# A mixture-of-experts layer on one core: the router chain reordered, the PLE product moved into the expert loop

## The reference

```python
h = rmsnorm(x, g_ffn)
logits = h @ w_router + b_router                # (256, 32)
top_val, top_idx = lax.top_k(logits, 4)
top_w = softmax(top_val)
for each expert e, for the tokens that chose it:
    gu = h[tok] @ w1[e] + b1[e]                 # w1[e] 1024 x 2048
    gate = min(gu[:, :1024], 7); lin = clip(gu[:, 1024:], -7, 7)
    y[tok] += top_w * (((lin + 1) * gate * sigmoid(1.702 * gate)) @ w2[e] + b2[e])
x = x + y
x = x + sigmoid(rmsnorm(x, g_ple) @ w_ple_gate) * (p @ w_ple)      # the PLE term
```

## Time and profile before

| | |
|---|---|
| three runs | 1286.07, 1288.97, 1289.33 us; median 1288.97 |
| the profiled execution | 1289.37 us, its span 1287.1 us |
| PE, DVE, ACT, POOL busy | 90%, 22%, 16%, 3% of the span |
| mean granted PE clock | 0.984 |
| HBM read | 446.71 MB |

### The profile page before, as it was taken

The page is one execution under the profiler, slowest core; times in us unless marked ns, Lnnn a source line. Parts: engine busy times, 40 slices in busy tenths (PEclk is TensorE's granted clock), DMA queues, the critical chain, the costliest instruction groups (busy, mean ns, idle before and its releaser), DMA issues. The chain is left out here.

```text
span 1287.1 us, 15903 instructions
## 1 busy us (share of the span) xinstructions
PE 1164.7 (90%) x6370; PEld 479.2 (37%) x6370; DVE 281.4 (22%) x787; ACT 212.0 (16%) x430; POOL 34.1 (3%) x49
## 2 busy tenths in 40 slices
PE   7999999989999989899899999888988999989868
PEld 4455544444343333333333333333333333333333
DVE  1474533272121111112111111111111111111121
ACT  2323435022111111111111111111111111111110
POOL 2221100000000000000000000000000000000000
PEclk9999999997999999999999999999999999999989
DMA  9835041971999999999999999999999999999920
GB/s 294 290 131 196 1 131 54 378 291 39 429 428 429 427 431 428 428 429 427 430 429 428 429 427 430 428 429 429 427 430 428 429 429 427 430 428 429 429 87 33
DMA packets 51003, 448.07 MB, mean 348 GB/s; under 512 B 9233, under 2 KB 11638, under 8 KB 26310
## 3 DMA queue, kind: packets, MB, share of 16 engines
q1 hardware_dynamic: 49534, 442.24, 82.7%
q0 software_dynamic: 1264, 5.27, 1.2%
q10 hardware_dynamic: 184, 0.29, 0.1%
HBM read 446.71 MB, written 4.22 MB: 350 GB/s over the span
## 5 line engine op out<-in xcount | busy, mean ns | idle before, releaser
L340 PE MATMUL ps<-ring,wbuf 128*64 128x512 f32 x2048 | 464.4, 598 | 67.4 <-DMA ring<-in_w_e 67.0
L340 PEld LDWEIGHTS ps<-ring,wbuf 128*64 128x64 f32 x2048 | 139.9, 137 | 374.1 <-issue 229.0
L364 PE MATMUL ps<-ring,wbuf 128*64 128x512 f32 x1024 | 226.8, 595 | 21.6 <-ACT wbuf L379 21.6
L413 DVE TENSOR_SCALAR wbuf<-ps 128x512 f32<-128x512 f32 x32 | 22.1, 692 | 748.2 <-PE ps L340 748.2
L364 PEld LDWEIGHTS ps<-ring,wbuf 128*64 128x64 f32 x1024 | 70.7, 137 | 155.6 <-issue 127.9
L375 ACT ACTIVATE wbuf<-wbuf 128x512 f32<-128x512 f32 x32 | 20.1, 630 | 511.5 <-DVE wbuf L413 511.5
L1099 PE MATMUL ps<-wbuf,hT 128*128 128x512 f32 (+2 forms) x224 | 85.4, 540 | 1.0 <-ACT hT L571 1.0
L325 PE MATMUL ps<-wbuf 64*128 64x512 f32 x264 | 65.6, 615 | 0.7 <-ACT wbuf L381 0.7
L1181 PE MATMUL ps<-wbuf,hT 128*128 128x512 f32 x128 | 62.6, 619 | 0.0
L1099 PEld LDWEIGHTS ps<-wbuf,hT 128*128 128x128 f32 x224 | 42.1, 190 | 41.1 <-issue 37.9
L381 ACT COPY wbuf<-ps 128x512 f32<-128x512 f32 x32 | 18.8, 586 | 230.0 <-PE ps L364 230.0
(11 more groups left out here) (233 smaller groups left out, 699.9 us busy)
## 6 DMA issues: line engine op xcount, KB each, us to landing
ring<-in_w_e SPq DMA_DIRECT2D x192, 2048.0 KB, 24.3
wbuf<-in_w_in SPq DMA_DIRECT2D x9, 2048.0 KB, 9.0
wbuf<-in_w_out SPq DMA_DIRECT2D x1, 4096.0 KB, 14.1
rel_rows_repeated<-rel_rows POOLq DMA_DIRECT2D x1, 3072.0 KB, 20.7
wbuf<-in_w_ple_gate SPq DMA_DIRECT2D x1, 3072.0 KB, 17.5
ring<-rel_rows_repeated POOLq DMA_DIRECT2D x1, 2048.0 KB, 10.9
wbuf<-in_w_branch_a SPq DMA_DIRECT2D x2, 1024.0 KB, 9.8
wbuf<-in_w_branch_b SPq DMA_DIRECT2D x1, 2048.0 KB, 17.8
```

The lines of the kernel that those rows point to most:

```text
L340: l = mm((G, Lb)[n // 2][(n % 2) * SLOTS:(n % 2 + 1) * SLOTS, :], xeT[:, k, :], ring3[:, i, r * 2 * DFF + n * 512:r * 2 * DFF + (n + 1) * ...
L364: l = mm(O[n * SLOTS:(n + 1) * SLOTS, :], actT[:, r, h * SLOTS:(h + 1) * SLOTS], ring3[:, i, r * DM + n * 512:r * DM + (n + 1) * 512], sta ...
L413: d.tensor_scalar(gc, ps[0][:, :], LIMIT, None, ALU.min).then_inc(s["gc_ready"], 1)
```

## The change

The attention part, the last part after the loop and all sizes stay. In the stretch between:

- `g_ffn` is multiplied once into the router weights `wr` on DVE; the eight small ACT evacuations of a tile become two plain copies (`x_copy`).
- Residual add, squares and the split into parts go by halves of 512. ACT makes part 0 straight from `x` with the scale (`hi`) and part 1 (`mid`), DVE the remainders and part 2. POOL keeps one instruction, `pow`.
- PE does `x_rows(1)`, `router(0)` and `x_rows(2)` ahead of `w_out(3)`.
- The mask comes from `match_replace` on the top four (`choose`), the rank counts are bfloat16 products. Exponential and `Wt` come after the one-hot matrix of expert 0.
- `b_e2` is loaded into the rows of `oe`, and the first visit's scatter adds it; DVE sets the four output banks to zero instead (`y_init`), after the first `take_rows`.
- The PLE product runs between the twelfth and the thirteenth visit (`ple_pe`, `ple_act`), so the loop is written twice, for 12 and for 20 visits.
- SP: `w_ple_gate` is loaded in 5/8 and 3/8 in place of 6/8 and 2/8, the later part behind `rt_ps` 2 and `hp_ready` 4.

The core of the diff:

```diff
@@ expert_pe @@
+            if a is first:
+                te.wait_ge(wt_ready, 1)
+                for t in range(TT):
+                    l = tr(T[:, t * P:(t + 1) * P], Wt[:, t, :], ident)
+                l.then_inc(s["wst_ps"], 1)
...
+            if a is first:
+                te.wait_ge(y_init, 1)
+                with te.Fori(0, PLE_AFTER) as it:
+                    visit(it)
+                ple_pe(te)
+                with te.Fori(PLE_AFTER, NE) as it:
+                    visit(it)
...
+        def ple_pe(te):
+            te.wait_ge(ld_p, 16)
+            for k in range(2):
+                for t in range(TT):
+                    l = tr(ps[3][:, k * SEQ + t * P:k * SEQ + (t + 1) * P], pin[:, t, k * P:(k + 1) * P], ident)
+            l.then_inc(pt_ps, 1)
+            te.wait_ge(pt_ev, 1)
+            te.wait_ge(ld_ple, 16)
+            for i in range(4):
+                t, n = i // 2, (i % 2) * 512
+                if i == 3:
+                    te.wait_ge(pl_ev, 1)
+                for k in range(2):
+                    l = mm(ps[(0, 1, 3, 0)[i]][:, :], pT[:, k, t * P:(t + 1) * P], wple[:, k, n:n + 512], start=k == 0, stop=k == 1)
+                l.then_inc(pl_ps, 1)
+            te.wait_ge(pl_ev, 4)
@@ expert_dve @@
             take_rows()
+            if a is first:
+                ve.wait_ge(t_ev, NT + 8)
+                for b in range(4, 8):
+                    l = d.memset(ps[b][:, :], 0.0)
+                l.then_inc(y_init, 1)
@@ sync @@
+                for n in range(2):
+                    sp.dma_start(oe[n * SLOTS:n * SLOTS + NE, :], io["b_e2"][0][:, n * 512:(n + 1) * 512]).then_inc(ld_be2, 16)
...
-                sp.wait_ge(hp_ready, 2)
-                sp.dma_start(wple_g[:, 0:2], w_gate[:, 0:2]).then_inc(ld_ple_gate, 16)
+                sp.wait_ge(rt_ps, 2)
+                sp.wait_ge(hp_ready, 4)
+                sp.dma_start(wple_g[:, 0:3], w_gate[:, 0:3]).then_inc(ld_ple_gate, 16)
@@ scalar @@
+                for n in range(4):
+                    merged_copy(n)
+                x_copy(0)
+                x_copy(1)
+                hi(0)
+                mid(0)
+                x_copy(2)
+                x_copy(3)
+                hi(1)
+                mid(1)
                 sc.wait_ge(lg_ready, 1)
...
+                a.activation(ex, lgx, ACT.Exp).then_inc(rt_exp, 1)
@@ vector @@
+                d.tensor_tensor(wr, wr, bc(gT[:, 16:24], NE), ALU.mult).then_inc(wr_ready, 1)
...
+                def choose(t):
                     ve.wait_ge(rt_ps, t + 1)
                     ch(d.scalar_tensor_tensor(lg[:, t, :], ps[6 + t][:, 0:NE], rs[:, t:t + 1], br, ALU.mult, ALU.add))
                     ch(d.max(top8[:, t, :], lg[:, t, :]))
+                    ch(d.tensor_scalar(lgx[:, t, :], lg[:, t, :], top8[:, t, 0:1], None, ALU.subtract))
+                    ch(d.memset(top8[:, t, TOPK:8], -TAKEN))
+                    ch(d.match_replace(lg[:, t, :], top8[:, t, :], lg[:, t, :], TAKEN))
+                    d.tensor_scalar(Mb[:, t, :], lg[:, t, :], (BLOCKED + TAKEN) / 2, None, ALU.is_lt).then_inc(m_ready, 1)
+
+                add(0)
+                add(1)
+                square(0)
+                square(1)
+                add(2)
+                square(2)
+                for n in range(2):
+                    remainder(0, n)
+                for n in range(2):
+                    last_part(0, n)
+                choose(0)
+                add(3)
+                square(3)
+                remainder(1, 0)
+                remainder(1, 1)
+                choose(1)
+                last_part(1, 0)
+                last_part(1, 1)
+                ve.wait_ge(m_ready, 2)
+                d.tensor_copy(Mt, Mb).then_inc(lg_ready, 1)
...
@@ tensor @@
                 w_out(2)
                 x_rows(0)
+                x_rows(1)
+                te.wait_ge(wr_ready, 1)
+                router(0, range(KT))
+                x_rows(2)
                 w_out(3)
-                x_rows(1)
-                x_rows(2)
...
+                router(1, range(4))
                 x_rows(3)
+                router(1, range(4, KT))
+                te.wait_ge(m_ready, 2)
```

More of the change, by code:

```diff
@@ L329, in expert_pe, with visit @@
             gather()
-            with te.Fori(0, a["visits"]) as it:
+            if a is first:
[3 more added lines that the diff above has]
+                l.then_inc(s["wst_ps"], 1)
+            def visit(it):
                 te.wait_ge(s["sel_ready"], it + 1)
@@ L366, in expert_pe @@
                     l.then_inc(s["pieces_used"], 1)
+            if a is first:
[5 more added lines that the diff above has]
+                    visit(it)
+            else:
+                with te.Fori(0, a["visits"]) as it:
+                    visit(it)
             te.wait_ge(s["out_ready"], a["visits"] + 1)
@@ L381, in expert_act @@
                 nc.scalar.copy(oe, ps[2][:, :]).then_inc(s["out_ready"], 1)
+            if a is first:
+                with sc.Fori(0, PLE_AFTER) as it:
+                    visit(it)
+                ple_act(sc)
+                with sc.Fori(PLE_AFTER, NE) as it:
+                    visit(it)
+            else:
+                with sc.Fori(0, a["visits"]) as it:
+                    visit(it)
         def expert_dve(ve, a):
@@ L696, in _, with merged_copy @@
                     a.activation(gates[:, t, :], gates[:, t, :], ACT.Sigmoid).then_inc(gates_ready, 1)
[L697 to L703, removed]
+                def merged_copy(n):
                     k = NT + n
@@ L707, in _, with x_copy @@
                     a.copy(hTv[:, k0:k0 + 4, t * P:(t + 1) * P], ps[4 + k % 2][:, :].rearrange("p (k t) -> p k t", k=4)).then_inc(t_ev, 1)
-                part(1, 0, 1)
-                part(2, 0, 2)
-                for n in range(4):
+                def x_copy(n):
                     k = NT + 4 + n
@@ new lines, in add, with square @@
+                def add(i):
+                    t, c = i // 2, slice((i % 2) * 512, (i % 2 + 1) * 512)
+                    ve.wait_ge(wo_ps, i + 1)
+                    d.tensor_tensor(x[:, t, c], ps[i][:, :], x[:, t, c], ALU.add).then_inc(x2_ready, 1)
+                def square(i):
+                    t, c = i // 2, slice((i % 2) * 512, (i % 2 + 1) * 512)
+                    ve.wait_ge(x2_ready, i + 1)
+                    l = d.tensor_tensor_reduce(out=xr[t][:, c], in0=x[:, t, c], in1=x[:, t, c], scale=1.0 / DM,
+                                               scalar=EPS if i % 2 == 0 else sm2[:, t, 0:1],
+                                               op0=ALU.mult, op1=ALU.add, accum_out=sm2[:, t, 0:1] if i % 2 == 0 else ssx[:, t:t + 1])
+                    if i % 2 == 0:
+                        ch(l)
+                    else:
+                        l.then_inc(f_sq, 1)
@@ new lines, in _ @@
+                ve.wait_ge(m_ready, 2)
+                d.tensor_copy(Mt, Mb).then_inc(lg_ready, 1)
+                ve.wait_ge(lg_ready, 1)
+                ve.wait_ge(rk_ps, 1)
+                ch(d.scalar_tensor_tensor(rank[:, :, 0:NE], ps[7][:, P:P + TT * NE].rearrange("p (t e) -> p t e", t=TT), 1.0, Mt, ALU.add, ALU.mult))
+                i1 = iota1[:, 0, :]
+                for t in range(TT):
+                    l = d.tensor_scalar(S[:, t, :], i1, rank[:, t, 0:1], None, ALU.is_equal)
+                l.then_inc(first["s"]["s_ready"], 1)
@@ L1013, in _ @@
-                ve.wait_ge(wt_ready, 1)
-                second_remainder(1)
-                ve.wait_ge(rk_ps, 1)
                 for t in range(TT):
-                    ch(d.scalar_tensor_tensor(rank[:, t, 0:NE], ps[7][:, t * NE:(t + 1) * NE], 1.0, Mt[:, t, :], ALU.add, ALU.mult))
+                    l = d.tensor_scalar(Wt[:, t, :].rearrange("p (r e) -> p r e", r=ROUNDS), bm(ex[:, t, :], ROUNDS), sm2[:, t, 1:2], None, ALU.mult)
+                l.then_inc(wt_ready, 1)
+                for t in range(TT):
```

195 lines of the change are left out of this document (75 added, 120 removed).

## The result

| | before | after |
|---|---|---|
| median of five runs | 1289.33 us (1286.07 to 1290.23) | 1277.39 us (1274.59 to 1281.20) |
| ratio | | 0.9913, 95% interval 0.9894 to 0.9931 |
| profiled execution, span | 1289.37, 1287.1 us | 1279.43, 1277.6 us |

The change makes the kernel 0.9% faster, between 9 and 14 us by the interval. A second set of six runs gave 1277.07 and a ratio of 0.9902 (0.9879 to 0.9924). The forecast was 1275.0, within 1270.7 to 1280.8: the direction and the range hold, and the point is 2.4 us too low.

The account below looks back on a forecast made before the run. The chain up to the first used piece of expert 1, then the even weight stream, sets the end. 14.8 us earlier less 0.45 for the clock gives 1289.37 - 14.35 = 1275.0 us, range 1270.7 to 1280.8.

Parts of the forecast that it names:

- rival of a slower stream: In the loop the stream's rate falls; 0.6 us more a visit gives 1293.6 us; chance 3%.
- that of no gain: Something other than the first used piece starts the stream, so the earlier chain is swallowed: 1289 us; chance 4%.
- Step 1: Chain up to the end of `w_out(3)`: it ends at 283.3 us, 4.2 us later than before.
- the clock falls earlier: Clock falls at the start of `w_out(3)`, which ends 1.9 to 2.8 us later: 1276.9 to 1277.8 us; chance 10%.
- Step 2: From the end of `w_out(3)` to the gather: 7.75 us, gather starting at 291.05 instead of 307.77.
- Step 3: From the gather to the first piece: zeroings 1.95 us, L340 at 297.25 instead of 312.03, 14.8 us earlier.
- Step 4: PE's clock at the first piece: starts at the lower level, rises 4.6 us after the start; 0.45 us lost.
- Step 5: PLE product in the loop: PE uses no piece for 9.1 us, hidden by queued loads; cost nothing.
- lead of 16.9: Smallest time in the loop from a piece's issue to its own transfer's start, 16.9 us, more than 9.1.
- The handover: Two stalls of 5.1 us as PE leaves one loop and enters the other: 1277.4 us; chance 6%.
- Step 6: Transfers ahead of the loop: last 1.5 MB of `w_ple_gate` done by about 297 us, `b_e2` needed near 312; cost nothing.
- 14.35: Net gain forecast up to the first piece, in us: 14.8 from the earlier chain less 0.45 for the clock.

Follow-up runs that it names:

- fourfold product: Changed kernel with three more PLE products (24 logical products, results overwritten) in the gap after the twelfth visit; median 1287.18 us, ratio to before 0.9992.
- second profile: Profiled execution of the changed kernel run once more with no edit; median of that set 1277.07 us, ratio to before 0.9902.
- first profile: Profiled execution of the changed kernel in its first measurement, 1279.43 us; median of that set 1277.39 us, ratio to before 0.9913.
- the same with filling: Kernel before with the PLE product moved into the loop and fifteen unread products of constants in PE's gaps; median 1278.88 us, ratio to before 0.9915.

## Why the prediction was right

- **The bound was right.** Every profile has the same loop, 922.7 to 923.4 us, whatever lies ahead of it, but for the fourfold product. So the end of the loop moves with the first load, microsecond for microsecond; what follows it took 46.8 to 47.5 us in nine profiles, and 2 to 4 less in four. The rival of a slower stream didn't come, nor that of no gain.
- **Step 1** gave the end of `w_out(3)` as 12.6 us after the load of `p`. It was 12.64 in the second profile, 15.8 in the first. The difference is the rival *the clock falls earlier*, which had 10%: `router(0)` took 2.87 us instead of 1.94, `w_out(3)` 2.0 us more. Together with `x_rows(2)` that is 3.2, above the rival's 1.9 to 2.8, since the clock fell before `w_out(3)` and not at its start. It is the largest term between the forecast and the first profile, and comes in some executions only: of the five profiles with this order and no filling ahead of `w_out(3)`, two show it.
- **Step 2** gave 7.75 us to the gather; 7.9 in both profiles.
- **Step 3** gave 6.2 us from the gather to L346; 6.9 in both. The gather was wholly at the lower clock (2.83 to `take_rows` instead of 2.56), and the zeroing added 2.4 between `take_rows` and the bias product, not 1.95: the instructions took 2.11, less than the upper bound of 2.8.
- **Step 4** gave 5.7 us for the first piece; 5.84 and 6.11. The mechanism was right and its cost 0.2 and 0.4 too small; that the gather too runs at the lower level was not counted. Of the two rises that it read before, one lies 5.7 us (297.9) and not 5.5 behind the start of PE's work.
- **Step 5 was right.** PE used no piece for 9.4 us. The loop grew by 0.2 us, and the fourfold product puts what is covered at some 15.2 us, 1.7 less than the lead of 16.9. (The sum of the lead holds for the piece directly ahead in the queue, which landed at 693.06; the text says two ahead. The third slot's load was issued at 662.63, so its lead is 20.6.) PE regained 3.1 us a visit, not 2.5. The timeline of the gap:

```profile
636.92 3.76 SPq L299 DMA_DIRECT2D ring<-in_w_e  x2
640.11 0.66 PE L393 MATMUL ps<-misc,oT 128*128 128x128 f32 x4
...
641.44 7.13 PE L402 MATMUL ps<-wbuf,oT 128*128 128x512 f32 x16 [0.68 <-ACT oT L408]
...
648.61 0.58 ACT L411 COPY hT<-ps 128x512 f32<-128x512 f32 x1 [1.13 <-PE ps L402]
649.53 0.62 PE L340 MATMUL ps<-gat,misc 96*64 96x512 bf16 x4 [0.96 <-ACT hT L411]
649.96 6.63 PE L346 MATMUL ps<-ring,wbuf 128*64 128x512 f32 x30
```

- **The handover** did not stall: the transposes follow the last `w_e2` product at once, and the second loop begins 0.34 us after ACT's last copy. By the rule of the Trainium skill ("Runtime: NRT & Kernel Launch", Instruction fetch mechanics) a branch out of the resident pages would wait for a fetch; none of these engine times shows a wait. The 5.1 us behind the loop, from which the rival took its price, are no fixed time: two profiles have 2.0.
- **Step 6 was right.** The loads of `w_ple_gate` and `b_e2` delayed nothing.

Where the 14.35 went: the second profile gives 46.59 - 33.55 = 13.0, short by 1.3, which is 0.7 of step 3, 0.45 of step 4 and small terms; the first gives 10.1, short by 2.9 more, the early fall of the clock. What the sum could not tell is which part of the change gives what. Moving the PLE product alone gives 4.4 of distance and no time; the same with filling gives 8.4 of distance and 0.85% of time, and in its profile 3.3 us of the time were saved behind the loop. The change took both the PLE product and the `b_e2` product off the chain, and so left no long product there to run slowly. That its gain comes from the two together is argued from these profiles and not shown: no run took the `b_e2` product off alone. How often the clock falls ahead of `w_out(3)` stays open. The executions scatter over 1274.59 to 1281.20, wider than the 2.4 us by which the point was missed; that it came so near is in part luck.

## What to carry to other kernels

Where a load stream at an even rate is the bound, look for the moment that starts it: the chain ahead of it counts in full, and work inside it is free up to about the smallest lead of a load over its transfer (here 9.4 us cost nothing, and of 30.0 us some 15.2). Before taking work out of TensorE's queue in a stretch of short waits, read the granted clock there: the work may be followed by a rise of the clock that goes with it, and what remains on the chain then runs at half speed (the `b_e2` product, 7.16 us instead of 3.69). When an order is changed to hide one piece of work, count what it delays as well: `router(0)` ahead of `w_out(3)`, to hide what follows from it, delayed the last projection by 3.9 us and the gather by 2.4. Compare the times of several executions and not one profile of each alone: moving the PLE product alone shortened the distance by 4.4 us in the profiles and the times by nothing.

## What was not expected of the hardware

In the run with the PLE product moved alone PE was busy without a break from 297.96 to 305.0 with products of 32 rows by 512 columns, and the clock stayed at the 1.2 GHz level all through, until 308.4; in the first profile of the changed kernel `w_out(3)`, with 128 rows and equally without a break, began at that level at 277.72, and the clock rose at 281.8, before it ended. In the kernel before and in the filled version the same product ran at the upper level (3.69 and 3.67 us), and the clock fell just behind it (at 308.1 and 298.3). Busy time in the profile is thus not a sure sign that the clock is held; whether it is the 32 rows was not tried.

ACT's copy with scale 0 into a PSUM bank took 0.56 us a piece (1.12 for two), about as DVE's zeroing of one (0.53).
